# Down weights of eight experts: four neighbouring rows in each partition, and the inner features taken with a step of four

## The chip, the cores and the metric

The kernel runs on one core of a Trainium2 chip. The metric is the device time of one execution in microseconds (us). All weights and activations are float32. The weights lie in the chip's memory (HBM) and are copied by DMA into the on-chip memory of 128 partitions, where TensorE reads them.

## The reference, cut to what matters

Two layers of a trunk are computed for 256 tokens of 1024 features; each has a token mixer and a feed-forward part. The feed-forward part of the second layer is a mixture of eight experts, and each token goes to its two best ones:

```
for e in range(N_EXPERTS):                       # 8 experts, FFN_EXPERT = 3584 inner features
    y = y + combine[:, e:e+1] * ((silu(t @ w_gate[e]) * (t @ w_up[e])) @ w_down[e])
```

`w_gate[e]` and `w_up[e]` are 1024 x 3584, `w_down[e]` is 3584 x 1024. The last product sums over the 3584 inner features, so their order is free as long as the hidden values and the rows of `w_down` follow the same one.

## The kernel before, in words

**The ring.** All large weights pass through one tensor `ring` of 7 slots (`SLOTS`), 2 MiB each: 128 partitions with 4096 float32 in each. SyncE's queue (`sp_program`) issues one DMA for each chunk in a fixed order. Ahead of each it waits on `freed`, which counts the chunks that TensorE has finished reading; TensorE waits on `landed[s]` ahead of the first use of a slot. A chunk of `w_gate` or `w_up` has all 1024 input features and 512 of the inner ones (`slot_up`: 128 partitions x 8 x 512): its contiguous runs in HBM are 2048 bytes. A chunk of `w_down` has 512 inner features and all 1024 outputs (`slot_down`: 128 partitions x 4 x 1024): partition p gets the rows p, 128 + p, 256 + p and 384 + p of the chunk's 512, four runs of 4096 bytes. Other matrices of `down` form (`attn_out`, `down`, `mlstm_out`) go through `weights` and are not touched.

**The experts.** One expert, fixed by its place (`FIRST`), comes first (`expert`, here with one tile of tokens): 7 steps over chunks of 512 inner features. In `step` the tokens are stationary and the weights move (L1692, L1695), which gives hidden values with the tokens in the partitions; ScalarE and VectorE make them `hx`; `turn` transposes them by TensorE in four blocks of 128 features (L1703); `down` multiplies by the down chunk (L1742). The other seven are handled in two groups ordered by how many tokens they have (`group`, four and three experts). The first of a group is "wide": its weights are stationary, 128 x 128 at a time, and the tokens move (L1838, 208 columns in the first group and 176 in the second), so hidden values come with features in the partitions and need no transpose; L1896 is its down product. The others are "narrow": tokens stationary, weights moving, then a transpose (L1877) and the down product. With up to 64 tokens the two halves of TensorE's columns take gate and up (L1861, L1864, down L1916); with up to 32 ("slim") the four quarters take two halves of gate and two of up, each 256 moving columns (L1854, down L1906). A *unit* is one chunk of 512 inner features of one expert: a gate, an up and a down chunk. The first group has 28 units (7 wide, 7 of 64 tokens, 14 slim), the second 21 (7 wide, 14 slim). Which unit comes when is set by `WIDE_AFTER`; TensorE runs the down product of a unit two units behind its gate and up, and SyncE's order (`group_order`) follows the same pattern: gate and up of unit s, then down of unit s - 2.

```python
                for u, part in group_order(g):
                    c = GROUP_CHUNK[g][(u, part)]
                    sp.wait_ge(freed, c + 1)
                    group_chunk(sp, members[UNITS[g][u].member], UNITS[g][u].round, part, c)
```

The branches with other shapes (`hidden_tile`, `any_group`) are in the program for other token counts and do not run with these inputs.

Of the kernel before, what the change touches and what calls it, by code (L numbers as in the profile page):

```python
# [28 lines left out]
P = 128  # L29
D = 1024  # L30
KT = D // P
S = 256
# [27 lines left out]
DK = SLOT // D  # L60
# [65 lines left out]
EJ = FE // WC  # L126
# [8 lines left out]
HALF = P // 2  # L135
# [105 lines left out]
def trunk(nc, a, out):  # L241
    with ExitStack() as ctx:
# [375 lines left out]
            eng.wait_ge(landed[i % SLOTS], 16 * (i // SLOTS + 1))  # L618


        def expert_chunk(sp, e, c):

            s = ring_place(c) % SLOTS
            n_up = 2 * EJ
            if c < n_up:
                w = a["moe_w_gate"] if c % 2 == 0 else a["moe_w_up"]
                src = w[0][e].rearrange("(k p) n -> p k n", p=P)[:, :, (c // 2) * WC:(c // 2 + 1) * WC]
                if c in ASIDE:
                    parts = aside[ASIDE.index(c)]
                    n = KT // len(parts)  # L630
                    for i, part in enumerate(parts):
                        sp.dma_start(part, src[:, i * n:(i + 1) * n]).then_inc(aside_landed[ASIDE.index(c)], 16)
                else:
                    sp.dma_start(slot_up(s), src).then_inc(landed[s], 16)
            else:
                j = c - n_up
                src = a["moe_w_down"][0][e].rearrange("(k p) n -> p k n", p=P)[:, j * DK:(j + 1) * DK, :]
                sp.dma_start(slot_down(s), src).then_inc(landed[s], 16)

        def group_chunk(sp, e, r, part, c):  # L640

            s = c % SLOTS
            if part < 2:
                w = a["moe_w_up"] if part else a["moe_w_gate"]
                src = w[0][e].rearrange("(k p) n -> p k n", p=P)[:, :, r * WC:(r + 1) * WC]
                sp.dma_start(slot_up(s), src).then_inc(landed[s], 16)  # L646
            else:
                src = a["moe_w_down"][0][e].rearrange("(k p) n -> p k n", p=P)[:, r * DK:(r + 1) * DK, :]
                sp.dma_start(slot_down(s), src).then_inc(landed[s], 16)  # L649

        def sp_program(sp):

# [477 lines left out]
        def pe_program(pe):  # L1130
# [513 lines left out]
            def expert(e, width):  # L1644
# [53 lines left out]
                def turn(j, chunks_read):  # L1698
                    pe.wait_ge(hx_ready, step_count(e, j))
                    if j >= 2:  # L1700
                        pe.wait_ge(turn_free, step_count(e, j - 2))
                    for c in range(STEP):
                        ins = pe.transpose(ps[:, 6 + j % 2, c * P:(c + 1) * P], hx[:, j % 2, c * P:(c + 1) * P], ident[:])  # L1703
                        if c == 0 and chunks_read:

                            ins.then_inc(freed, chunks_read)
                    ins.then_inc(turn_full, STEP)

                def hidden_tile(ft):


                    j, c = ft // STEP, ft % STEP
                    if c == 0:
                        arrived(2 * j)
                        arrived(2 * j + 1)
                    if ft >= UB:
                        pe.wait_ge(hx_ready, ft_count(e, ft - UB))
                    for half in range(2):
                        dst = ps[:, ft % UB, half * S:half * S + width]
                        for k in range(KT):  # L1720
                            if ft == half == 0 and k >= KT // 2 and k % 2 == 0:
                                pe.wait_ge(xg_ready, taken + k // 2 + 1)
                            ins = pe.matmul(dst, up_weights(2 * j + half, k)[:, c * P:(c + 1) * P], xg[:, k, 0:width], start=(k == 0), stop=(k == KT - 1))
                            if half == 0 and k == 0 and c == 0 and j:
                                ins.then_inc(freed, ring_chunks(j - 1))
                    ins.then_inc(step_full, 1)
# [58 lines left out]
            def group(g, w, slim):  # L1785
# [35 lines left out]
                def step(s):  # L1821
                    u = units[s]

                    def gathered(k):
                        if s == 0 and g == 0:
                            pe.wait_ge(group_x, max(k, u.fill % UB + UB) + 1)
                        elif s == k == 0:
                            pe.wait_ge(mulled, extra_fills(0, "near")[-1] + 1)

                    if u.wide:  # L1830
                        for half in range(2):
                            weights_in = arrived(s, half)
                            for ft in range(STEP):
                                if half == 0 and u.fill + ft >= UB:
                                    pe.wait_ge(mulled, u.fill + ft - UB + 1)
                                dst = ps[:, (u.fill + ft) % UB, half * S:half * S + w]
                                for k in range(KT):
                                    ins = pe.matmul(dst, weights_in[:, k, ft * P:(ft + 1) * P], xq[:, k, BASE:BASE + w],  # L1838
                                                    start=(k == 0), stop=(k == KT - 1))
                                    if ft == k == 0:  # L1840
                                        free_owed(ins)
                                if half:
                                    ins.then_inc(filled, 1)
                            owed[0] += 1
                        return
                    wg, wu = arrived(s, 0), arrived(s, 1)
                    first = HALF * (u.member - 1)
                    if u.fill >= UB:
                        pe.wait_ge(mulled, u.fill - UB + 1)
                    for k in range(KT):  # L1850
                        gathered(k)
                        if is_slim(u):
                            for q in range(4):
                                ins = pe.matmul(ps[QUARTER * q:QUARTER * (q + 1), u.fill % UB, 0:S],  # L1854
                                                xq[:, k, first:first + QUARTER], (wg, wu)[q // 2][:, k, q % 2 * S:(q % 2 + 1) * S],
                                                start=(k == 0), stop=(k == KT - 1))
                                if k == q == 0:
                                    free_owed(ins)
                        else:
                            x_k = xq[:, k, first:first + HALF]  # L1860
                            ins = pe.matmul(ps[0:HALF, u.fill % UB], x_k, wg[:, k, :], start=(k == 0), stop=(k == KT - 1))  # L1861
                            if k == 0:
                                free_owed(ins)
                            ins = pe.matmul(ps[HALF:P, u.fill % UB], x_k, wu[:, k, :], start=(k == 0), stop=(k == KT - 1))  # L1864
                    ins.then_inc(filled, 1)
                    owed[0] += 2

                def turn(s):
                    u = units[s]
                    pe.wait_ge(mulled, u.fill + 1)  # L1870
                    if u.turn >= 2:
                        pe.wait_ge(copied, u.turn - 1)
                    if s >= 2:
                        pe.wait_ge(added, units[s - 2].down + units[s - 2].downs)
                    pe.wait_ge(group_scat, 2 * (g + 1))
                    for c in range(STEP // 2 if is_slim(u) else STEP):
                        ins = pe.transpose(ps[:, 6 + u.turn % 2, c * HALF:(c + 1) * HALF],  # L1877
                                           hn[0:HALF, u.turn % 2, c * P:(c + 1) * P], ident[0:HALF, 0:HALF])
                        if c == 0:
                            free_owed(ins)  # L1880
                    ins.then_inc(turned, 1)
# [122 lines left out]
            def any_group(g):  # L2004
# [27 lines left out]
                def step(s):  # L2032
# [5 lines left out]
                    for ft in range(STEP):  # L2038
                        if s:
                            pe.wait_ge(any_hidden, STEP * (base + s - 1) + ft + 1)  # L2040
                        for half, ws in enumerate(weights_in):
                            for k in range(KT):
                                ins = pe.matmul(ps[:, ft, half * S:half * S + w], ws[:, k, ft * P:(ft + 1) * P],
                                                xa[:, k, offset[i]:offset[i] + w], start=(k == 0), stop=(k == KT - 1))
                                if ft == half == k == 0:
                                    free_owed(ins)
                        ins.then_inc(any_full, 1)
# [909 lines left out]
```

## Time and profile before

| | |
|---|---|
| time, median of 3 runs | 1594.16 us (1593.05 to 1594.63) |
| profiled execution: span from the first to the last instruction | 1592.0 us |
| moved by DMA over the span | 483.48 MB, mean 304 GB/s |
| TensorE busy | 1494.6 us, 94% of the span |
| mean granted TensorE clock | 0.980 of 2.4 GHz |

The span is that of one profiled execution; the median of the runs lies 2.2 us above it. TensorE's busy time counts a matmul from its start to its modelled end, and neighbours overlap, so 94% does not say that the engine runs at its peak. "PEld" is TensorE's loading of the stationary operand, which runs beside the matmuls. "DMA share" is the mean busy share of the 16 DMA engines; packets overlap a little, so a full queue shows as 1.03 or 1.04. A float32 product is two instructions on TensorE, so counts of matmuls are twice what the loops issue.

### The profile page before, as it was taken

The page shows a single profiled execution, that of the slowest core. Times are in us where ns is not written, and L with a number is a line of the kernel's source. Part 1 is how long each engine was busy: PE and PEld are TensorE (multiplying, and loading weights), DVE is VectorE, ACT ScalarE, POOL GpSimd, SP SyncE. Part 2 cuts the span into 40 slices and gives each one's busy share as a digit, 9 for nine tenths or more (in the row PEclk, how much of TensorE's full clock was granted, in tenths as well). Part 3 has the DMA queues.
Part 4 walks back from the last instruction along what each step waited for, and adds up shares of the span by engine and source line. Part 5 has one row for each costly group of instructions (what it writes and reads, how often), then busy time and mean ns, then how long its engine had stood idle before and what let it go on. Part 6 is the DMA issues. An engine that isn't in the chain of part 4 may idle for free.

```text
span 1592.0 us, 21871 instructions
## 1 busy us (share of the span) xinstructions
PE 1494.6 (94%) x9550; PEld 1089.1 (68%) x9550; DVE 510.3 (32%) x1061; ACT 163.3 (10%) x436; POOL 38.3 (2%) x84
## 2 busy tenths in 40 slices
PE   6998999999999899999999999999897899988987
PEld 4865588884487676443377877777774688876974
DVE  1388336366656455141211111111012211111014
ACT  1006210000110121031010000000000000000000
POOL 1000000000011000010000000000000000000000
PEclk9999999999999999999999999999999999999998
DMA  9996229769432010859999999999999999999994
GB/s 353 370 393 247 103 89 365 289 218 358 160 136 82 25 54 0 317 213 397 397 349 393 395 393 395 393 395 392 395 374 398 388 374 395 393 394 393 395 393 186
DMA packets 205824, 483.48 MB, mean 304 GB/s; under 512 B 4242, under 2 KB 6699, under 8 KB 205715
## 3 DMA queue, kind: packets, MB, share of 16 engines
q1 hardware_dynamic: 204736, 481.32, 80.9%
q8 instruction: 81, 1.33, 0.3%
q10 hardware_dynamic: 978, 0.61, 0.2%
q14 instruction: 29, 0.23, 0.0%
HBM read 480.86 MB, written 1.05 MB: 303 GB/s over the span
## 4 chain that ended last, share of the span: by engine, by line
PE 78%; DMA 10%; SPq 4%; DVE 3%; issue 3%; ACT 2%; POOL 0%; ACTq 0%; DVEq 0%; POOLq 0%
PE ps L1257 20%; PE ps L1838 13%; PE ps L1896 8%; DMA ring<-in_moe_w_gate 7%; PE ps L1244 5%; PE ps L1854 4%; PE ps L1421 4%; PE ps L1692 3%; PE ps L1861 3%; SPq L649 2%; PE ps L1906 2%; PE ps L1318 2%; DMA ring<-in_moe_w_down 2%; PE ps L1742 2%; SPq L646 1%
## 5 line engine op out<-in xcount | busy, mean ns | idle before, releaser
L1257 PE MATMUL ps<-hT,ring 128*128 128x256 f32 x1456 | 321.4, 381 | 3.1 <-issue 1.4
L1257 PEld LDWEIGHTS ps<-hT,ring 128*128 128x128 f32 x1456 | 274.6, 190 | 45.7 <-issue 6.6
L1838 PE MATMUL ps<-arena,ring 128*128 128x208 f32 (+1 forms) x1792 | 294.0, 326 | 4.2 <-DMA ring<-in_moe_w_gate 4.2
L1838 PEld LDWEIGHTS ps<-arena,ring 128*128 128x128 f32 x1792 | 291.2, 190 | 6.9 <-DMA ring<-in_moe_w_gate 6.5
L1896 PE MATMUL ps<-arena,ring 128*128 128x208 f32 (+1 forms) x896 | 149.3, 327 | 1.5 <-DMA ring<-in_moe_w_down 1.5
L1896 PEld LDWEIGHTS ps<-arena,ring 128*128 128x128 f32 x896 | 145.2, 190 | 2.6 <-DMA ring<-in_moe_w_down 1.8
L1854 PE MATMUL ps<-ring,arena 128*32 128x256 f32 x1792 | 115.4, 415 | 31.7 <-issue 31.7
L1854 PEld LDWEIGHTS ps<-ring,arena 128*32 128x32 f32 x1792 | 63.9, 120 | 81.2 <-issue 52.1
L2735 DVE TENSOR_TENSOR arena<-arena,ps 128x256 f32<-128x256 f32 x56 | 23.6, 422 | 274.1 <-ACT arena L990 274.1
L2142 DVE SCALAR_TENSOR_TENSOR arena<-ring,cond,arena 128x512 f32<-128x512 f32 x140 | 105.2, 752 | 5.0
L2753 DVE TENSOR_TENSOR arena<-arena,ps 128x512 f32<-128x512 f32 (+1 forms) x78 | 47.2, 606 | 141.0 <-PE ps L1896 96.3
L1244 PE MATMUL ps<-ring,arena 128*128 128x512 f32 x192 | 83.1, 593 | 1.3 <-DVE arena L2405 1.3
L2739 DVE TENSOR_TENSOR arena<-arena,ps 64x256 f32<-64x256 f32 (+1 forms) x35 | 16.7, 476 | 185.5 <-ACT arena L995 185.5
L1244 PEld LDWEIGHTS ps<-ring,arena 128*128 128x128 f32 x192 | 36.2, 190 | 45.5 <-issue 45.5
L1861 PE MATMUL ps<-ring,arena 128*64 128x512 f32 x112 | 53.7, 636 | 8.3 <-issue 8.3
L990 ACT ACTIVATE arena<-ps 128x256 f32<-128x256 f32 x56 | 21.5, 383 | 359.5 <-PE ps L1838 359.5
L1906 PE MATMUL ps<-ring,arena 128*32 128x256 f32 x896 | 53.9, 381 | 0.0
L1864 PE MATMUL ps<-ring,arena 128*64 128x512 f32 x112 | 53.8, 636 | 0.0
L995 ACT ACTIVATE arena<-ps 64x256 f32<-64x256 f32 (+1 forms) x35 | 14.7, 420 | 355.2 <-PE ps L1854 259.1
L1861 PEld LDWEIGHTS ps<-ring,arena 128*64 128x64 f32 x112 | 15.8, 147 | 41.9 <-issue 41.9
L728 POOL TENSOR_TENSOR small<-small 128x1 f32<-128x1 f32 (+1 forms) x20 | 12.5, 624 | 1323.6 <-DVE small L2722 892.8
L1695 PE MATMUL ps<-ring,arena 128*64 128x512 f32 x96 | 42.5, 595 | 0.0
(378 smaller groups left out, 1290.1 us busy)
## 6 DMA issues: line engine op xcount, KB each, us to landing
ring<-in_moe_w_down SPq DMA_DIRECT2D x56, 2048.0 KB, 19.2
ring<-in_moe_w_gate SPq DMA_DIRECT2D x55, 2048.0 KB, 19.3
ring<-in_moe_w_up SPq DMA_DIRECT2D x55, 2048.0 KB, 20.7
ring<-in_mod_w SPq DMA_DIRECT2D x24, 2048.0 KB, 15.3
ring<-in_mlstm_w_in SPq DMA_DIRECT2D x8, 2048.0 KB, 9.7
ring<-in_attn_w_in SPq DMA_DIRECT2D x6, 2048.0 KB, 20.5
ring<-in_ffn_w_gate SPq DMA_DIRECT2D x5, 2048.0 KB, 13.3
ring<-in_ffn_w_up SPq DMA_DIRECT2D x5, 2048.0 KB, 12.8
```

The source lines that it names most:

```text
L1244: ins = pe.matmul(ps[:, 4 + 2 * t + c], lhs[:, first + k, t * P:(t + 1) * P], w[:, k, c * 512:(c + 1) * 512], start=(first + k == 0), stop ...
L1257: ins = pe.matmul(dst, w[:, k, c * P:(c + 1) * P], hT[:, k, :], start=(k == 0), stop=(k == KT - 1))
L1421: return pe.matmul(seventh(m), left, right, start=(p == 0), stop=(p == PAIRS - 1))
L1692: ins = pe.matmul(ps[0:width, b], x_k, up_weights(2 * j, k), start=(k == 0), stop=(k == KT - 1))
L1838: ins = pe.matmul(dst, weights_in[:, k, ft * P:(ft + 1) * P], xq[:, k, BASE:BASE + w], start=(k == 0), stop=(k == KT - 1))
L1854: ins = pe.matmul(ps[QUARTER * q:QUARTER * (q + 1), u.fill % UB, 0:S], xq[:, k, first:first + QUARTER], (wg, wu)[q // 2][:, k, q % 2 * S:( ...
L1861: ins = pe.matmul(ps[0:HALF, u.fill % UB], x_k, wg[:, k, :], start=(k == 0), stop=(k == KT - 1))
L1864: ins = pe.matmul(ps[HALF:P, u.fill % UB], x_k, wu[:, k, :], start=(k == 0), stop=(k == KT - 1))
L1896: ins = pe.matmul(ps[:, 4 + b, half * S:half * S + w], wd[:, k, dt * P:(dt + 1) * P], ehw[u.round % 2][:, k, 0:w], start=(k == 0), stop=(k ...
L1906: ins = pe.matmul(ps[QUARTER * q:QUARTER * (q + 1), 4 + u.turn % 2, 0:S], ehn[:, u.turn % 2].rearrange("p k s -> p (k s)")[:, first:first ...
L2142: ins = dve.scalar_tensor_tensor(out=acc, in0=w[:, k], scalar=cond[:, k, 31:32], in1=acc, op0=ALU.mult, op1=ALU.add)
L2753: dve.tensor_tensor(y, y, part, ALU.add).then_inc(added, 1)
```

## The change

A down chunk of an expert is laid so that partition p holds the rows 4p, 4p + 1, 4p + 2 and 4p + 3 of its 512: 16384 contiguous bytes in HBM and in the partition. Place k of a partition now means the inner features 4p + k instead of 128k + p, so wherever 128 inner features are taken as one block, they are now taken with a step of four: as columns of the stationary gate and up weights of a wide unit (L1838), as columns of the hidden values that are transposed (L1703, L1877), and as pairs out of every four moving columns in a slim unit (L1854). There the hidden values of one quarter hold pairs, and their transposes take every second column. The down products themselves read what they read before.

```diff
+        def following_rows(e, r):
+            return a["moe_w_down"][0][e].rearrange("(r p b) n -> r p (b n)", r=EJ, b=DK)[r]
+        def fourth(c):
+            return slice(c, c + DK * (P - 1) + 1, DK)
+        def two_fourths(w, q):
+            return w.rearrange("p (x b) -> p x b", b=DK)[:, :, 2 * q:2 * q + 2]
...
-                src = a["moe_w_down"][0][e].rearrange("(k p) n -> p k n", p=P)[:, j * DK:(j + 1) * DK, :]
-                sp.dma_start(slot_down(s), src).then_inc(landed[s], 16)
+                sp.dma_start(ring[:, s], following_rows(e, j)).then_inc(landed[s], 16)
...
-                src = a["moe_w_down"][0][e].rearrange("(k p) n -> p k n", p=P)[:, r * DK:(r + 1) * DK, :]
-                sp.dma_start(slot_down(s), src).then_inc(landed[s], 16)
+                sp.dma_start(ring[:, s], following_rows(e, r)).then_inc(landed[s], 16)
...
-                        ins = pe.transpose(ps[:, 6 + j % 2, c * P:(c + 1) * P], hx[:, j % 2, c * P:(c + 1) * P], ident[:])
+                        ins = pe.transpose(ps[:, 6 + j % 2, c * P:(c + 1) * P], hx[:, j % 2, fourth(c)], ident[:])
...
-                                    ins = pe.matmul(dst, weights_in[:, k, ft * P:(ft + 1) * P], xq[:, k, BASE:BASE + w],
+                                    ins = pe.matmul(dst, weights_in[:, k, fourth(ft)], xq[:, k, BASE:BASE + w],
...
-                                                xq[:, k, first:first + QUARTER], (wg, wu)[q // 2][:, k, q % 2 * S:(q % 2 + 1) * S],
+                                                xq[:, k, first:first + QUARTER], two_fourths((wg, wu)[q // 2][:, k], q % 2),
...
-                                           hn[0:HALF, u.turn % 2, c * P:(c + 1) * P], ident[0:HALF, 0:HALF])
+                                           hn[0:HALF, u.turn % 2, slice(c, S, 2) if is_slim(u) else fourth(c)], ident[0:HALF, 0:HALF])
```

The same two replacements stand in the branches that do not run here.

## Rows read from the trace of the kernel before

**Rows 1.** The page's 40 slices: busy tenths of the DMA engines.

```profile
DMA  9996229769432010859999999999999999999994
```

**Rows 2.** Windows by stretch: busy us and instructions by engine, PEclk, DMA share, GB/s.

```profile
828.00:832.00 4.00, 4.00 (x45) 3.17 (x48) 0.76 (x2) 0.77 (x2) 0.00 (x0) 1.00 0.20 38
832.00:1120.00 288.00, 274.67 (x2112) 215.00 (x2106) 38.58 (x77) 16.76 (x47) 0.00 (x0) 0.98 1.04 393
1120.00:1161.00 41.00, 41.00 (x214) 34.64 (x211) 4.29 (x7) 1.90 (x5) 0.00 (x0) 0.94 1.04 393
1161.00:1165.00 4.00, 4.00 (x42) 3.20 (x44) 0.84 (x2) 0.77 (x2) 0.00 (x0) 1.00 0.67 231
1165.00:1216.00 51.00, 44.00 (x417) 27.05 (x413) 10.52 (x18) 2.42 (x7) 0.00 (x0) 0.98 1.04 392
1216.00:1282.00 66.00, 58.66 (x455) 43.02 (x448) 16.52 (x36) 3.43 (x9) 0.00 (x0) 0.92 1.04 393
1282.00:1286.00 4.00, 4.00 (x61) 2.64 (x63) 0.42 (x1) 0.55 (x2) 0.00 (x0) 1.00 0.66 201
1286.00:1540.00 254.00, 235.93 (x2184) 208.26 (x2180) 35.93 (x70) 15.01 (x45) 0.00 (x0) 0.98 1.04 394
1540.00:1566.00 26.00, 25.18 (x250) 18.46 (x245) 6.50 (x11) 1.35 (x5) 0.00 (x0) 0.91 1.03 398
```

**Rows 3.** Windows: only down chunks move in the first, only gate and up in the second.

```profile
740.00:770.00 30.00, 30.00 (x141) 10.38 (x138) 4.14 (x14) 2.32 (x5) 0.00 (x0) 1.00 1.03 409
776.00:802.00 26.00, 24.32 (x79) 9.02 (x79) 7.63 (x11) 0.59 (x1) 0.00 (x0) 0.93 1.05 386
```

**Rows 4.** The page's DMA queues: packets, MB, share of 16 engines.

```profile
q1 hardware_dynamic: 204736, 481.32, 80.9%
```

**Rows 5.** Chain of waits around 1120 us: start us, us, what.

```profile
1113.95 5.50 issue
...
1140.88 22.51 PE ps L1838 x128
```

**Rows 6.** Chain of waits from 1200 to 1283 us.

```profile
1210.07 5.50 issue
...
1251.61 5.60 issue
...
1263.90 19.09 PE ps L1838 x128
```

**Rows 7.** Chain of waits near the end.

```profile
1535.74 4.07 issue
1539.81 6.01 PE ps L1854 x64
...
1555.83 3.59 PE ps L1854 x64
```

**Rows 8.** Down chunks issued from L649 in 832:1090, 1163:1196 and 1284:1515 (min/median/max ns).

```profile
L649 SPq DMA_DIRECT2D ring<-in_moe_w_down x17: 373/5084/6182, 835.8 to 1088.1; - x17
...
L649 SPq DMA_DIRECT2D ring<-in_moe_w_down x3: 373/4105/5119, 1163.8 to 1185.4; - x3
...
L649 SPq DMA_DIRECT2D ring<-in_moe_w_down x15: 373/4970/5967, 1287.8 to 1508.4; - x15
```

**Rows 9.** Loads of the stationary operand by form: shapes, count, busy us, mean ns, idle before.

```profile
L1838 PEld LDWEIGHTS ps<-arena,ring 128*128 128x128 f32 x1792 | 291.2, 190 | 6.9 <-DMA ring<-in_moe_w_gate 6.5 <-issue 0.4
...
L1877 PEld LDWEIGHTS ps<-ident,arena 64*128 64x128 f32 x84 | 7.8, 137 | 15.8 <-issue 15.8
...
L1703 PEld LDWEIGHTS ps<-ident,arena 128*128 128x128 f32 x28 | 2.9, 141 | 5.7 <-issue 5.7
...
L1176 PEld LDWEIGHTS ps<-ident,arena 48*128 48x128 f32 x8 | 1.0, 201 | 0.0
```

**Rows 10.** Timeline at 65 us and at 1239 us: start us, us over all, what.

```profile
64.90 0.98 PEld L1176 LDWEIGHTS ps<-ident,arena 48*128 48x128 f32 x8
...
1239.21 3.76 PEld L1952 LDWEIGHTS ps<-hT,arena 128*128 128x128 f32 x32
```

More of the change, by code:

```diff
@@ L1722, in hidden_tile @@
                                 pe.wait_ge(xg_ready, taken + k // 2 + 1)
-                            ins = pe.matmul(dst, up_weights(2 * j + half, k)[:, c * P:(c + 1) * P], xg[:, k, 0:width], start=(k == 0), stop=(k == KT - 1))
+                            ins = pe.matmul(dst, up_weights(2 * j + half, k)[:, fourth(c)], xg[:, k, 0:width], start=(k == 0), stop=(k == KT - 1))
                             if half == 0 and k == 0 and c == 0 and j:
@@ L2042, in step @@
                             for k in range(KT):
-                                ins = pe.matmul(ps[:, ft, half * S:half * S + w], ws[:, k, ft * P:(ft + 1) * P],
+                                ins = pe.matmul(ps[:, ft, half * S:half * S + w], ws[:, k, fourth(ft)],
                                                 xa[:, k, offset[i]:offset[i] + w], start=(k == 0), stop=(k == KT - 1))
```

## The prediction

> **What bounds the kernel now.** I read the page's slices first. From the 19th slice on, at about 716 us, all DMA engines are busy to the end but for the last slice [rows 1]: this is the stage of the experts. TensorE is nearly always busy there too, so the slices alone don't say which of the two sets the pace. The windows by stretch do. The engines' share is 1.04, at 392 to 394 GB/s, in the five long stretches up to 1540, and it falls in three short ones, at 828, 1161 and 1282 us [rows 2]. In those TensorE is busy for the whole 4 us: it holds the ring's slots, SyncE has nothing it may issue, and the DMA queue runs dry. In the long stretches it is the other way round: TensorE idles 13.3 us of 288 (832 to 1120), 7.0 of 51 (1165 to 1216) and 18.1 of 254 (1286 to 1540) [rows 2]. The chain of waits names what it waits for there. TensorE stands 5.50 us until 1119.45, again 5.50 us from 1210.07, and 4.07 us from 1535.74 [rows 5 to 7], each time ahead of a narrow unit, which needs a whole gate chunk and a whole up chunk; 5.5 us is what one such chunk takes (below). So the experts' stage is a race in which DMA leads most of the time, and TensorE takes over in stretches that end in a dry queue:
>
> - up to 832 us TensorE sets the time (the queue is dry at 828);
> - 832 to 1119.5 DMA sets it; from there to the dip at 1161 to 1165, TensorE;
> - 1165 to 1215.6 DMA; from 1215.6 to the dip at 1282 to 1286, TensorE, with a change of group at 1251.61 that costs 5.60 us without a transfer in the chain [rows 6];
> - 1286 to 1539.8 DMA; from 1539.8 on TensorE and VectorE, with what is left [rows 7].
>
> A faster transfer is worth something only in the three DMA stretches, 832 to 1119.5, 1165 to 1215.6 and 1286 to 1539.8. What it gains elsewhere is given back at the next dry queue, since the dip ends when TensorE frees a slot.
>
> **What the down chunks cost now and after.** In a window where only down chunks move the rate is 409 GB/s, where only gate and up move 386 [rows 3]. 2,097,152 bytes take 5.13 us at the one and 5.43 at the other. The share is about the same, so the engines were full in both. What differs is the length of the runs, 4096 bytes against 2048. The queue's count fits one packet per run: 160 chunks of 1024 runs and 66 of 512, with the smaller transfers and 16 completion packets a DMA, come near the 204736 that the page counts [rows 4]. So 512 packets fewer save 0.30 us, 0.59 ns of wall time each with all 16 engines at work, or 9.4 ns on the one engine. With 16384 bytes in one piece a chunk has 128 packets, 384 fewer: 384 x 0.59 = 0.225 us less, 4.90 us, 428 GB/s. That extends a line of two lengths by a factor of four in length; the bounds are nothing (if a long run is cut into pieces of 4096 bytes, or if 409 GB/s is a limit of the memory) and the 0.31 us that would be left if packets cost nothing at all. I take 0.225.
>
> The Trainium skill, "DMA: Bandwidth & Descriptors", section "Why small descriptors are slow (HBM only)", gives a fixed cost of some three cycles a packet and 32 bytes of metadata a transfer, and holds packing small ones together worth it only up to 256 bytes. An estimate from that page is 4.7 ns a packet on its engine, half of what the rows show; the sum below would be 4 us in place of 7.9.
>
> How many chunks count: 17 down chunks issued from 835.8 to 1088.1 land in the first DMA stretch (a landing comes some 19 us behind its issue), 3 issued from 1163.8 to 1185.4 in the second, 15 issued from 1287.8 to 1508.4 in the third [rows 8]. 35 x 0.225 = 7.9 us. The other 21 of the 56 down chunks land where TensorE sets the time. Can TensorE follow? It has to give up 17 x 0.225 = 3.8 us of its 13.3 idle, 0.7 of 7.0 and 3.4 of 18.1. It can.
>
> **SyncE's queue.** Nothing is moved in it. An issue of L649 now takes 5.1 us in the median and 0.37 at the least [rows 8], so the queue below is full and SyncE stands until there is room. A chunk of 128 packets leaves more room, SyncE will stand less, and nothing comes of it: it is already ahead of the transfers.
>
> **The wide units' stationary operand (L1838).** Now 128 neighbouring columns are loaded, then every fourth, one per 16 bytes. No such product is in the trace, but a transpose with a wide step is. L1176 loads 128 columns that lie 32 bytes apart, in 201 ns, where L1703 and L1877 load neighbours in 141 and 137 [rows 9]. The step costs 60 ns there. But a product's load is not a transpose's: with neighbours it already takes 190 ns [rows 9]. What counts is how long it occupies the load path. Eight loads of L1176 take 0.98 us, or (0.98 - 0.20) / 7 = 111 ns apart; 32 of L1952, ordinary products with 128 moving columns, (3.76 - 0.19) / 31 = 115 ns apart [rows 10]. So a column costs under 0.9 ns in both, and I read it as one limit: a load with a step runs at the pace at which an ordinary float32 load runs anyway. A wide product takes 22.51 us / 128 = 176 ns in the first group and 19.09 / 128 = 149 in the second [rows 5, 6]. 115 ns lies beneath either, with 34 ns to spare. Value taken: 0. Upper bound: the load is slowed as often as the transpose's, 115 to 230 ns, and becomes the pace (first rival).
>
> The Trainium skill, "SBUF — State Buffer", section "Specifications (TRN2)", speaks against the change here: reads are at full rate only with two hits or more on each 16-byte line. The transposes' 60 ns agree; whether a float32 product, slower to begin with, still feels it, no row shows. By that rule the case is the first rival below.
>
> **The slim units' moving operand (L1854).** 64 of them take 3.59 us at the full clock [rows 7]: 56 ns apart, four at a time, so 224 ns for 256 columns, 0.88 ns a column. After the change each 16 bytes give two of the four columns. One column per 16 bytes was delivered in 0.87 ns above, so two per 16 bytes should cost nothing. Lower bound 0; upper bound, if the four streams share one reader and each 16 bytes count, twice 3.59 us in all 28 slim units.
>
> **The transposes.** The 28 of L1703 lie in the first expert, where TensorE sets the time. Each four wait for the first load, 60 ns longer; the rest run under 128 moving columns. 7 x 0.06 = 0.4 us, at most 28 x 0.06 = 1.7. Of the 84 of L1877 the 28 of the 64-token units step by 16 bytes and 56 by 8. All 84 at 60 ns would be 5.0 us; but I place only about a quarter, some 20, in TensorE's own stretches, so up to 1.2 us, and I take half, 0.6. Together 1.0 us on the path, between 0 and 2.9.
>
> **Sum.** 1592.0 - 7.9 + 1.0 = 1585.1 us of span. The median of the runs is 2.2 us above the span: 1587.3. There may be 2.4 us more: L1854 takes 6.01 us behind the 4.07 us wait and 3.59 later [rows 7], because the granted clock was at its half level there, 1.2 GHz of 2.4, for part of the stretch (0.91 in the mean of 1540 to 1566) [rows 2]. With the wait some 1 us shorter it may not fall. I do not count on it.
>
> **The rivals.**
>
> - *The stepped load becomes the pace (slower).* Place: L1838. It decides when a load occupies more than 149 ns in the second group, 176 in the first. At 230 ns a wide unit loses 128 x 54 = 6.9 us in the first group and 128 x 81 = 10.4 in the second. TensorE's stretches take it whole: one unit at 807, one at 1140.9, one at 1263.9, together 24 us. Five units between 832 and 1120 take 34.5 less the 13.3 idle, 21; six between 1286 and 1540 take 62 less 18, 44. Nothing is left of the DMA gain: 1594.2 + 89 + 1, about 1684. If 60 ns are only added (175), the first group doesn't feel it; the second loses 3.3 a unit: one in full, and six, 20 us, over 18 us of idle, which costs 2 and the 3.4 gained there: 1587.3 + 3.3 + 5.4 = 1596. For it: the step's price in transposes. Against: the two spacings. 8 in 100 for both.
> - *The slim products slow (slower).* At twice 3.59 us, about eight lie in TensorE's own stretches: 29 us, 1616 or more. 4 in 100.
> - *Long runs read worse (slower).* Sixteen engines each in a 16384-byte piece may meet in the memory more than now. If a down chunk falls to the rate of the gate chunks, 35 x 0.30 = 10.5 us: 1594.2 + 10.5 + 1 = 1605.7. Every run length in the trace speaks against it. 6 in 100.
> - *The transfer does not get faster (same).* Pieces of 4096 bytes again, or a limit at 409 GB/s: 1594.2 + 1.0 = 1595.2. 15 in 100.
> - *The forecast*, with more or less of the 7.9: 67 in 100.
>
> **Range and chances.** The forecast's own range is from 35 x 0.31 = 10.9 with transposes free and the clock kept, 1594.2 - 10.9 - 2.4 = 1580.9, to half of the 7.9, should the line through two lengths bend, with transposes dear, 1594.2 - 3.9 + 2.9 = 1593.2. Taking in the unchanged transfer gives 1582 to 1596. A measurement here tells about 0.2%, 3.2 us. Faster: 67 of the forecast less 3 for a gain under 3.2 us, 64. Same: 15, these 3, and 3 of the added 60 ns, 21. Slower: 15.
>
> **What would show it.** In a window of down chunks alone the rate should be near 428 GB/s at a share near 1.03, with a quarter as many packets per chunk; the page's queue should count 56 x 384 = 21504 packets fewer. The loads of L1703 should take some 200 ns. L1838 may load in 190 to 200 ns and must still show 128 in 22.5 and 19.1 us, L1854 64 in 3.59. The dips at 828, 1161 and 1282 should be longer and TensorE's idle in the DMA stretches smaller. Wrong would be: packets still of 4096 bytes, or a wide product over 176 and 149 ns.

## The result and the profile after

The change makes the kernel 5.7% slower: 1684.61 us (median of 4 runs, 1684.01 to 1686.05) against 1593.61 before (median of 4, 1592.56 to 1594.63), ratio 1.0572 with a 95% interval of 1.0559 to 1.0585. The profiled execution spans 1684.3 us.

In the changed kernel's file the lines named before stand ten or eleven further down: L1838 is L1848, L1854 is L1864, L1896 is L1906, L1877 is L1887, L1703 is L1713.

First the page's slices and its queue, which answer to [rows 1, 4]:

```profile
DMA  9994259866421107599799899899899789898974
...
q1 hardware_dynamic: 183232, 481.32, 76.2%
```

There are 204736 - 183232 = 21504 packets fewer, which is what 56 chunks with 384 fewer each come to. But the DMA engines are no longer full: from the 19th slice on the digits dip every few slices.

The windows by stretch answer to [rows 2] and to the first window of [rows 3]. Columns as there: busy us by engine (PE, PEld, DVE, ACT, POOL), granted clock, DMA share, GB/s.

```profile
740.00:770.00 30.00, 30.00 (x144) 10.70 (x142) 4.83 (x15) 3.09 (x7) 0.00 (x0) 1.00 1.01 428
...
832.00:1120.00 288.00, 288.00 (x1952) 233.65 (x1952) 36.62 (x73) 16.85 (x45) 0.00 (x0) 1.00 0.93 352
...
1165.00:1216.00 51.00, 51.00 (x353) 43.87 (x351) 5.29 (x10) 2.54 (x7) 0.00 (x0) 1.00 0.85 321
1216.00:1320.00 104.00, 91.47 (x666) 64.53 (x665) 24.24 (x48) 4.25 (x12) 0.00 (x0) 0.93 1.01 385
1320.00:1632.00 312.00, 312.00 (x2249) 285.60 (x2252) 36.76 (x72) 17.43 (x49) 0.00 (x0) 1.00 0.88 330
```

The first window holds down chunks alone: 428 GB/s, the rate that was forecast, in place of 409. What follows is the loss. From 832 to 1120 and from 1320 to 1632 TensorE is busy for every microsecond and the DMA share is 0.93 and 0.88. TensorE waits for weights only around 1248. In the kernel before DMA led most of the race between the two; now TensorE leads it.

Loads of the stationary operand by form answer to [rows 9]. L1906, the wide units' down product, stands beside them as a load that the change leaves alone (count | busy us, mean ns | idle before):

```profile
L1848 PEld LDWEIGHTS ps<-arena,ring 128*128 128x128 f32 x1792 | 419.2, 330 | 2.5 <-issue 2.5
...
L1906 PEld LDWEIGHTS ps<-arena,ring 128*128 128x128 f32 x896 | 145.2, 190 | 0.9
...
L1887 PEld LDWEIGHTS ps<-ident,arena 64*128 64x128 f32 x84 | 12.6, 205 | 15.4 <-issue 15.4
...
L1713 PEld LDWEIGHTS ps<-ident,arena 128*128 128x128 f32 x28 | 3.9, 209 | 5.7 <-issue 5.7
```

And the chain of waits (start us, us, what). It answers to [rows 5, 6], where 128 products of a wide unit took 22.51 us in the first group and 19.09 in the second:

```profile
1049.51 29.86 PE ps L1848 x128
...
1113.91 30.13 PE ps L1848 x128
...
1550.84 29.86 PE ps L1848 x128
```

A wide load with a step of 16 bytes takes 330 ns instead of 190, and a wide product 30.0 / 128 = 234 ns, whether 208 columns move behind it (the first two rows) or 176 (the third). The number of moving columns no longer matters, so the load sets the pace. Seven wide units of each group give TensorE 7 x (30.0 - 22.5) + 7 x (30.0 - 19.1) = 129 us more. It had 38.4 us of idle to give in the DMA stretches [rows 2] and gave all but the 5.25 us around 1248. That makes 96 us, where 91 were measured. The pages' totals give the same account for the two profiled executions: TensorE's busy time rose from 1494.6 to 1619.3 us, by 125, and its idle fell from 97.4 to 65.0, by 32; the span grew by the difference, 92. So the idle went as counted. The busy time grew by some 13 us less than the 129 and the 9 that the narrow units add (worked out under load_step4). Against that stands the granted clock, whose mean rose from 0.980 to 0.990: it is 1.00 in the windows above in which TensorE never stops, where it was 0.98 before [rows 2]. As an estimate, one hundredth of 1600 us is 16, so the clock can account for it; no run takes it apart.

### The profile page after: what moved, and what is told of

Read it like the earlier page. It is cut to its first block, busy times and chain, and to the rows that moved or that the text cites. A ratio compares the mean times of both kernels' runs of the same rounds, so it can differ in the third digit from the quotient of the medians.

```text
span 1684.3 us, 21871 instructions
## 1 busy us (share of the span) xinstructions
PE 1619.3 (96%) x9550; PEld 1219.2 (72%) x9550; DVE 510.2 (30%) x1061; ACT 165.6 (10%) x436; POOL 38.3 (2%) x84
## 3 DMA queue, kind: packets, MB, share of 16 engines
q1 hardware_dynamic: 183232, 481.32, 76.2%
## 4 chain that ended last, share of the span: by engine, by line
PE 92%; DVE 3%; ACT 2%; issue 1%; POOL 0%; DMA 0%; ACTq 0%; DVEq 0%; POOLq 0%
PE ps L1848 25%; PE ps L1267 19%; PE ps L1906 9%; PE ps L1864 6%; PE ps L1254 5%; PE ps L1431 4%; PE ps L1916 3%; PE ps L1702 3%; PE ps L1871 3%; PE ps L1328 2%; PE ps L1926 1%; PE ps L1752 1%; PE ps L1887 1%; PE ps L1947 1%; PE ps L1650 1%
## 5 line engine op out<-in xcount | busy, mean ns | idle before, releaser
L1848 PE MATMUL ps<-arena,ring 128*128 128x208 f32 (+1 forms) x1792 | 421.3, 397 | 0.0
L1848 PEld LDWEIGHTS ps<-arena,ring 128*128 128x128 f32 x1792 | 419.2, 330 | 2.5 <-issue 2.5
L1906 PE MATMUL ps<-arena,ring 128*128 128x208 f32 (+1 forms) x896 | 149.3, 327 | 0.0
L1906 PEld LDWEIGHTS ps<-arena,ring 128*128 128x128 f32 x896 | 145.2, 190 | 0.9
L1864 PE MATMUL ps<-ring,arena 128*32 128x256 f32 x1792 | 111.0, 399 | 10.8 <-issue 10.8
L1864 PEld LDWEIGHTS ps<-ring,arena 128*32 128x32 f32 x1792 | 59.4, 111 | 58.6 <-issue 20.5
L1916 PE MATMUL ps<-ring,arena 128*32 128x256 f32 x896 | 54.0, 381 | 0.0
L1871 PE MATMUL ps<-ring,arena 128*64 128x512 f32 x112 | 49.5, 595 | 1.6 <-issue 1.6
L1874 PE MATMUL ps<-ring,arena 128*64 128x512 f32 x112 | 49.6, 595 | 0.0
L1916 PEld LDWEIGHTS ps<-ring,arena 128*32 128x32 f32 x896 | 27.6, 109 | 21.1 <-issue 4.6
L1702 PE MATMUL ps<-ring,arena 128*64 128x512 f32 x96 | 42.5, 595 | 0.0
## 6 DMA issues: line engine op xcount, KB each, us to landing
ring<-in_ffn_w_gate SPq DMA_DIRECT2D x5, 2048.0 KB, 12.7
ring<-in_ffn_w_up SPq DMA_DIRECT2D x5, 2048.0 KB, 12.7
```

Source lines behind the costliest of these rows:

```text
L1702: ins = pe.matmul(ps[0:width, b], x_k, up_weights(2 * j, k), start=(k == 0), stop=(k == KT - 1))
L1848: ins = pe.matmul(dst, weights_in[:, k, fourth(ft)], xq[:, k, BASE:BASE + w], start=(k == 0), stop=(k == KT - 1))
L1906: ins = pe.matmul(ps[:, 4 + b, half * S:half * S + w], wd[:, k, dt * P:(dt + 1) * P], ehw[u.round % 2][:, k, 0:w], start=(k == 0), stop=(k ...
L1916: ins = pe.matmul(ps[QUARTER * q:QUARTER * (q + 1), 4 + u.turn % 2, 0:S], ehn[:, u.turn % 2].rearrange("p k s -> p (k s)")[:, first:first ...
```

## The experiments

The first four separate the suspects. Each starts from one of the two kernels. A cut inside a fence is marked with three dots.

**load_step4.** The kernel before, with one line changed:

```diff
-   ins = pe.matmul(dst, weights_in[:, k, ft * P:(ft + 1) * P], xq[:, k, BASE:BASE + w],
+   ins = pe.matmul(dst, weights_in[:, k, slice(ft, ft + 4 * (P - 1) + 1, 4)], xq[:, k, BASE:BASE + w],
...
```

> The kernel before, in which the wide units' gate and up loads alone take every fourth column (other columns than the reference needs, so the hidden values of the wide units are wrong); down chunks, transposes and slim products as before. Theory (a load with a 16-byte step occupies TensorE for some 235 ns in place of 115, and that alone makes the change slow): 128 of L1838 take 30 us in both groups, in all 129 us more on TensorE, of which 38 us of its idle in the three DMA stretches are used up: 1593.6 + 91 = about 1684, the load of L1838 shows 330 ns. Rival (the slow load comes with the 16384-byte pieces, which write a partition for longer while it is read): loads stay at 190 ns and the time at 1593.6.

Measured: 1677.53 us against 1593.78, ratio 1.0518 (1.0502 to 1.0534). The chain has 128 of L1838 at 29.87 and 30.13 us. The load's row in the page:

```profile
L1838 PEld LDWEIGHTS ps<-arena,ring 128*128 128x128 f32 x1792 | 419.2, 330 | 2.5 <-issue 2.5
```

It is the row of the changed kernel to the digit, with 4096-byte runs and not one packet fewer. The rival, that the long pieces slow the loads, falls. The stepped load by itself brings 84 of the 91 us; the sum had said 91.

The other 7 us lie in the narrow units' edits, which the changed kernel has besides, on a path that TensorE now sets nearly all the way. The chains of the two traces show them at the same place of the program, a slim product behind a down product of 1.86 us and then four transposes. First load_step4, then the changed kernel:

```profile
967.05 3.45 PE ps L1854 x64
970.51 0.39 PE ps L1877 x4
```

```profile
969.15 3.60 PE ps L1864 x64
972.76 0.62 PE ps L1887 x4
```

The slim product is 0.15 us longer and the four transposes 0.23; a slim unit's two transposes went from 0.27 to 0.38 (both chains). Over 28 slim units and 7 of 64 tokens that is 28 x (0.15 + 0.11) + 7 x 0.23 = 8.9 us of work, against 8.3 us between the two profiled spans (1676.0 and 1684.3).

**plain_load.** The changed kernel with the opposite edit, every other part of the change kept:

```diff
-   ins = pe.matmul(dst, weights_in[:, k, fourth(ft)], xq[:, k, BASE:BASE + w],
+   ins = pe.matmul(dst, weights_in[:, k, ft * P:(ft + 1) * P], xq[:, k, BASE:BASE + w],
...
```

> The changed kernel with the wide units' gate and up columns taken as neighbours again, all else as changed (the wide units' hidden values then meet the wrong down rows, so their part of the output is wrong). Theory: nothing but the stepped load was slow, so the forecast's sum returns: 35 down chunks at 0.225 us less, 7.9, and 1.0 for the transposes: 1593.6 - 6.9 = 1586.7, down chunks alone at 428 GB/s, loads of L1838 at 190 ns. Rival (16384-byte pieces slow the loads): loads stay at 330 ns and the time near 1684. Rival (stepped transposes and paired moving columns cost several us together): 1590 or more.

Measured: 1586.76 us, ratio 0.9958 (0.9944 to 0.9973). What made the kernel slow was this one line, and with the rest of the change it is 0.4% faster than before. The window of down chunks still shows 427 GB/s. Its row of the loads by form:

```profile
L1848 PEld LDWEIGHTS ps<-arena,ring 128*128 128x128 f32 x1792 | 291.8, 190 | 2.9 <-issue 1.6 <-DMA ring<-in_moe_w_gate 1.2
```

**load_step2.** As load_step4, with `slice(ft, ft + 2 * (P - 1) + 1, 2)`: two columns in each 16 bytes.

> As load_step4, with every second column (8-byte step, two columns in each 16 bytes); the wide units' hidden values are wrong. Theory A (any step costs): in the changed kernel transposes whose load steps by 8 bytes stand 98 ns apart, by 16 bytes 112, and 60 without a step, so the 8-byte step has 73% of the price; a wide load would occupy 115 + 0.73 x 120 = 203 ns, 128 take 26 us, TensorE gets 7 x 3.5 + 7 x 6.9 = 73 us more and gives up 38 of idle: about 1629. Theory B (two columns in each 16 bytes are enough for the full rate): 1593.6, loads of L1838 at 190 ns.

Measured: 1593.16 us, ratio 0.9997 (0.9986 to 1.0007). Theory B holds. Theory A, which carried the transposes' price over to products, is wrong. The load takes 197 ns, and 128 products still take 22.51 and 19.10 us:

```profile
L1838 PEld LDWEIGHTS ps<-arena,ring 128*128 128x128 f32 x1792 | 292.9, 197 | 5.8 <-DMA ring<-in_moe_w_gate 5.3 <-issue 0.4
```

```profile
1138.79 22.51 PE ps L1838 x128
1261.52 19.10 PE ps L1838 x128
```

**load_step3.** As load_step2, with every third column. It asks whether the price goes by the 16-byte pieces that a load touches.

> The kernel before with the wide units' loads at every third column (12-byte step; wrong hidden values of the wide units). Theory: a load pays for the 16-byte pieces that it touches, 1.84 ns each, or 0.9 ns a column, whichever is more. At a step of three, 4 columns lie in 3 pieces: 1.38 ns a column, 177 ns a load, so 128 products take 22.6 us in the first group (22.5 before) and 22.6 in the second (19.1 before), 25 us more on TensorE in all and some 18 of it under idle: about 1600, the load shows some 272 ns. Rival (a step above 8 bytes costs as a step of 16 does): 330 ns, 30 us and 1678.

Measured: 1596.87 us, ratio 1.0018 (1.0009 to 1.0027). 128 products take 22.51 us in the first group and 22.43 in the second (the chain's rows). The second group's pace is the load's, 22.43 / 128 = 175 ns, where 96 pieces at 1.84 ns are 177. The load's row shows 257 ns, where the expectation had 272. The time came out 3.5 us above before, less than the 6 expected. The second group's seven wide units have 7 x 3.3 = 23 us more work; the page has 12.7 us less idle of TensorE in all than before (84.7 against 97.4) and a mean clock of 0.985 against 0.980, so cover and clock took up more of it than the expectation's 18.

```profile
1263.87 22.43 PE ps L1838 x128
```

```profile
L1838 PEld LDWEIGHTS ps<-arena,ring 128*128 128x128 f32 x1792 | 317.0, 257 | 7.2 <-DMA ring<-in_moe_w_gate 5.9
```

The next two take the forecast's terms one at a time.

**rows_only.** The changed kernel's two `dma_start` lines and nothing else of the change.

> The changed kernel's down chunks (16384 bytes in each partition) alone, with every load, transpose and moving operand as before the change; hidden values meet the wrong down rows, so the experts' output is wrong. Theory: the transfer's term by itself, 35 x 0.225 = 7.9 us less: 1585.7. Rival: the term is smaller because TensorE follows only in part: 1588 or more.

Measured: 1585.71 us against 1593.40, ratio 0.9957 (0.9943 to 0.9971): 6.9 us by the ratio, 7.7 by the medians, with 7.9 expected.

**narrow_steps.** The kernel before with `fourth(c)` and `slice(c, S, 2)` in the transposes and `two_fourths` in the slim product.

> The kernel before with the changed kernel's stepped transposes and the slim units' paired moving columns, down chunks and wide loads as before; hidden values meet the wrong down rows, so the experts' output is wrong. Theory: 1.0 us on the path, between 0 and 2.9: 1594.6. Rival (they cost nothing that can be measured): 1593.6.

Measured: 1594.66 us, ratio 1.0008 (0.9999 to 1.0017): 1.3 us, with an interval that holds both the 1.0 expected and nothing. It doesn't tell the two apart, but it excludes the upper bound of 2.9. The edits do cost TensorE time (the rows under load_step4); the kernel's time shows little of it here, where DMA leads most of the way.

The last five compute the complete output. Four of them are meant to be faster.

**mixed.** The changed kernel, wide units as before (`wide` is handed to `group_chunk`):

```diff
+            elif wide:
+                src = a["moe_w_down"][0][e].rearrange("(k p) n -> p k n", p=P)[:, r * DK:(r + 1) * DK, :]
+                sp.dma_start(slot_down(s), src).then_inc(landed[s], 16)
             else:
                 sp.dma_start(ring[:, s], following_rows(e, r)).then_inc(landed[s], 16)
...
-   ins = pe.matmul(dst, weights_in[:, k, fourth(ft)], xq[:, k, BASE:BASE + w],
+   ins = pe.matmul(dst, weights_in[:, k, ft * P:(ft + 1) * P], xq[:, k, BASE:BASE + w],
...
```

> The changed kernel with the wide units as before (down chunk in four rows of 4096 bytes, neighbouring columns) and the first expert and all narrow units as changed. The output is complete. Theory: of the 35 down chunks that count some 25 belong to narrow units: 25 x 0.225 = 5.6 us, less 1.0 for the transposes: 1593.6 - 4.6 = 1589.0. Rival (the stepped transposes and the paired columns cost more than the chunks give): 1593 to 1596.

Measured: 1588.63 us, ratio 0.9966 (0.9954 to 0.9978).

**mixed_pairs.** As mixed, the wide chunk in pairs of rows, wide columns with a step of two:

```diff
+        def paired_rows(e, r):
+            return a["moe_w_down"][0][e].rearrange("(r h p b) n -> r p h (b n)", r=EJ, h=2, b=2)[r]
+        def second(c):
+            return slice(c // 2 * S + c % 2, c // 2 * S + c % 2 + 2 * (P - 1) + 1, 2)
...
+            elif wide:
+                sp.dma_start(half_pairs(s), paired_rows(e, r)).then_inc(landed[s], 16)
...
-   ins = pe.matmul(dst, weights_in[:, k, fourth(ft)], xq[:, k, BASE:BASE + w],
+   ins = pe.matmul(dst, weights_in[:, k, second(ft)], xq[:, k, BASE:BASE + w],
...
```

`half_pairs` is the slot as two runs of 2048 float32 in each partition.

> As mixed, but a wide unit's down chunk is laid with two neighbouring rows in each partition (runs of 8192 bytes) and its gate and up columns are taken with a step of two. Complete output. Theory: two columns in each 16 bytes load at 196 ns and hide under the products as in load_step2, and 256 packets fewer save 256 x 0.59 = 0.15 us a chunk on the ten wide chunks that count: 1.5 us less than mixed, 1587.1. Rival: no gain beyond mixed, 1588.6, since the load is a little longer.

Measured: 1586.10 us against 1593.52, ratio 0.9950 (0.9937 to 0.9964). It beats both kernels. That it beats mixed is not shown: the intervals overlap.

**all_pairs.** One layout for all units, pairs of rows; slim moving columns stay neighbours.

> The changed kernel with two neighbouring rows in each partition everywhere: runs of 8192 bytes, columns of wide loads and of transposes with a step of two, the slim units' moving columns as neighbours. Complete output. Theory: a chunk takes 4.98 us, 0.15 less than before, 35 x 0.15 = 5.3 us, less 1.0 for the transposes: 1593.8 - 4.3 = 1589.5. Rival (a load at one step of two costs some 200 ns as the transposes' do): near 1630.

Measured: 1587.33 us, ratio 0.9965 (0.9953 to 0.9977), and in the window of down chunks:

```profile
740.00:770.00 30.00, 30.00 (x137) 10.79 (x134) 4.23 (x15) 2.33 (x5) 0.00 (x0) 1.00 1.01 421
```

2,097,152 bytes at 421 GB/s take 4.98 us, which is what the prediction's price for a packet gives at this third length. The transposes step here but the slim products do not, and in this run's chain 64 slim products take 3.45 and 3.59 us, as without the change: the extra 0.15 us under load_step4 comes with the pairs.

**mixed_pairs_first.** As mixed_pairs, the first expert as before the change.

> As mixed_pairs, with the first expert as before (its down chunks in four rows, its transposes without a step). Complete output. Theory: the first expert lies where TensorE sets the time, so its faster chunks bring nothing and its 28 stepped transposes cost 0.4 us, at most 1.7: 1586.7. Rival (a faster transfer there frees the queue for the first group's chunks and is worth something): 1588 or more.

Measured: 1587.44 us, ratio 0.9953 (0.9939 to 0.9966). It can't be told from mixed_pairs, so the run doesn't decide between its theories.

**moving_step4.** As mixed, the slim units' moving columns one from each 16 bytes, so that their transposes take neighbours again:

```diff
-            return w.rearrange("p (x b) -> p x b", b=DK)[:, :, 2 * q:2 * q + 2]
+            return w.rearrange("p (x b) -> p b x", b=DK)[:, 2 * q:2 * q + 2, :]
...
```

> As mixed, but the slim units' moving columns are taken one from each 16 bytes (every fourth, then the next every fourth), so that their transposes take neighbours. Complete output. Theory A (the moving operand suffers from one column per 16 bytes as the loaded one does, 1.84 ns a column): a slim gate and up product takes 256 x 1.84 = 470 ns in place of 224, 64 take 7.5 us in place of 3.6, 28 slim units cost 109 us on TensorE less what idle is left (some 33 us): 1588.6 + 76 = 1665. Theory B (the moving operand takes a column per 16 bytes at its usual pace): 3.6 us and about 1588.

Measured: 1645.08 us, ratio 1.0323 (1.0304 to 1.0342). Theory A: 64 slim products (L1867 here) take 7.24 us in place of 3.59 [rows 7], 7.24 x 4 / 64 = 452 ns for 256 columns, 1.77 ns each. The expectation's total was 20 us too high. 7 of these are the products, 28 x 3.65 = 102 us more where 109 were expected. The cover was not larger than expected: between the pages of mixed and of this run TensorE's idle falls from 88.1 to 58.5 us, by 30 where 33 were counted. But its busy time grows by 89 only (1496.6 to 1585.2). The transposes give back 28 x 0.11 = 3 us of the 102, and the mean clock is 0.992 against 0.986; the rest was not divided further.

```profile
1227.23 7.24 PE ps L1867 x64
```

## Why the prediction was wrong

**The step that failed** is the price of the wide units' load, in the prediction's words "a load with a step runs at the pace at which an ordinary float32 load runs anyway", value taken 0. It is 234 - 115 = 119 ns for each of the 1792 loads of L1838; 85 ns of it show in the second group and 58 in the first. The rows were right and the reading of them wrong. L1176, a transpose's load with a step, stood 111 ns apart, and L1952, a product's load without one, 115 [rows 10]. I took two numbers that happened to be near for one limit. The comparison to make was like with like: a transpose with a step against a transpose without. Both are in the trace of before. L1172 takes every fourth column, 16 bytes apart, and L1877 neighbours, four loads each:

```profile
64.44 0.55 PEld L1172 LDWEIGHTS ps<-ident,arena 48*128 48x128 f32 x4 [0.33 <-issue]
```

```profile
830.21 0.32 PEld L1877 LDWEIGHTS ps<-ident,arena 64*128 64x128 f32 x4 [0.25 <-issue]
```

They stand (0.55 - 0.21) / 3 = 0.11 us apart and (0.32 - 0.14) / 3 = 0.06. In the changed kernel L1877's loads, then with a step of 16 bytes, show L1172's spacing:

```profile
839.77 0.55 PEld L1887 LDWEIGHTS ps<-ident,arena 64*128 64x128 f32 x4 [0.19 <-issue]
```

The 16-byte step makes a transpose's load occupy 1.9 times as long, and a product's, from 115 to 234, 2.0 times. So the factor was there to be read, as spacing; the mean durations of [rows 9], 201 ns against 137 and 141, show it only as 1.4 to 1.5. I used a doubling for the upper bound alone and gave that rival, with its milder form, 8 in 100.

**The Trainium skill's rule** was the one that decided. "SBUF — State Buffer", section "Specifications (TRN2)", wants two hits or more on each 16-byte line. For the loads of products the runs agree at each step tried: full pace at steps of one and two columns, 175 ns at three, 234 at four. For the loads of transposes they do not: with a step of two, two hits on each line, these stand 98 ns apart and not 60 (the 28 slim turns of the changed kernel against those of before).

**The first rival** gave 1684, with a load of 230 ns. Its mechanism is the one that the runs show; that its time is right to 1 us owes something to chance. It counted 24 us in TensorE's own stretches and 65 behind the idle, and 1 us for the transposes. The load was 234, one wait of 5.25 us stayed and the narrow units took some 9 us, which together is some 15 us more than it counted; about as much came back, most likely by the clock.

**The transfer** was right at each step. The chunk takes 4.90 us (428 GB/s), the queue counts 21504 packets fewer, and 35 chunks at 0.225 us are 7.9 us where rows_only measured 6.9 to 7.7. The Trainium skill's "DMA: Bandwidth & Descriptors", section "Why small descriptors are slow (HBM only)", by whose figures the estimate was 4 us, has the packet's cost too low for this case: chunks in 8192-byte runs at 4.98 us and in 16384-byte runs at 4.90 fit the 9.4 ns a packet of the rows. The two rivals on the transfer (no gain, worse reads) fall with the same windows.

**The slim units' moving operand** was taken at nothing, and that is nearly right: 64 products with pairs of columns take 0.15 us longer than with neighbours (3.60 against 3.45), 4%, or 4 us in all 28 slim units. The reason given was wrong here too ("one column per 16 bytes was delivered in 0.87 ns"); one column in each 16 bytes doubles the product, as moving_step4 shows, and it is the second column that makes it nearly free. **The transposes** were priced at 1.0 us on the path; narrow_steps has 1.3 for them and the pairs together, with an interval that reaches down to nothing. **The idle of TensorE** was counted rightly, but as cover for 7.9 us of gain, where it became cover for 129 us of loss.

## What to carry to other kernels

A layout that lengthens a transfer's runs is paid for where the data is read. Here 384 packets fewer a chunk are worth some 0.4%, and one float32 column in each 16 bytes of a stationary operand costs more than ten times that. Take a step of two (it stays hidden under 176 moving columns; a transpose's load does feel it), or keep the layout where the weights are stationary and change it where they move in pairs. When an operation is not in the trace, price it from two rows that differ in nothing but the property in question, as a factor, and check what the factor does to the operation that is slower to begin with, before two equal numbers are read as one limit.

## What the runs showed of the hardware

- Float32 loads of 128 columns for products, by the pace of the products behind them: at most 115 ns with neighbours, at most 149 with a step of two, 175 with three, 234 with four. The last two are 1.82 and 1.83 ns for each 16-byte piece touched.
- A moving operand with one column in each 16 bytes takes 1.77 ns a column, four streams at once, where neighbours take 0.88 at most. With two columns in each 16 bytes 64 products take 3.60 us where neighbours take 3.45.
- A transpose's load does not follow that count. It starts 60 ns behind the one before with neighbours, 98 with a step of 8 bytes (the 28 turns of slim units in the changed kernel) and 113 in the mean with a step of 16. So two columns a piece cost something here and one a piece costs less than the 234 ns of a product's load. Why stays open.
- Down chunks in runs of 4096, 8192 and 16384 bytes take 5.13, 4.98 and 4.90 us, which fits a straight line in the number of packets at 0.59 ns each, as far as windows that show whole GB/s can tell.
